# Inner order of the four products per contraction step in a two-feature-tile product (one core)

## The chip, the cores and the metric

The kernel runs on one core of a Trainium2 chip. The metric is the device time in microseconds, the median of the runs.

## The reference, cut to what matters

All arrays are float32. The model has 256 tokens of width 2048. Two layers of attention and MLP come first, then one layer with a recurrent unit (LRU) and a matrix LSTM, then one state-space (SSD) layer. The large products are the input projections and the MLP's first product:

```python
for l in range(DEPTH):                                   # DEPTH = 2
    h = rmsnorm(x, norm_mix[l]);  proj = einsum('bsd,de->bse', h, w_in[l])
    ...                                                  # three attentions
    x = x + einsum('bse,ed->bsd', mix, w_o[l])
    h = rmsnorm(x, norm_mlp[l]);  u = relu(einsum('bsd,df->bsf', h, w_up[l]))
    x = x + einsum('bsf,fd->bsd', u * u, w_down[l])      # u * u: 8192 wide
...
u = x @ w_in                                             # LRU + mLSTM layer
...
u = x @ w_in                                             # SSD layer
```

## The kernel before, in words

**Split operands.** Every float32 factor of a large product is kept as a high part and a low part, both in the engine's float32r form. A product is the sum high x high + high x low + low x high. The weights come from memory as units of 1 MB (`raw`, 128 x 2048), issued by the SyncE queue. ScalarE writes their high part (`whi`), VectorE the low part (`wlo`, line 1590 or 1597). Each of these tiles has four slots. TensorE then multiplies.

**The products of this change** (lines 2639 and 2641 in `products`, lines 2699 and 2701 in `feature_part`) have the weights as the stationary operand and the activations as the moving one. Call them H and L. One pass makes 256 output features, as two feature tiles f = 0, 1 of 128 each. Tile f has its own PSUM bank b + f. The contraction over 2048 has 16 steps kt of 128. In each step and for each f there are two products:

- H: the weights' high part, 128 x 128, against 512 columns: the 256 tokens of the activations' high part, and beside them the 256 of the low part. It fills the whole bank.
- L: the weights' low part, 128 x 128, against the 256 columns of the activations' high part. It is added to the second half of the same bank.

So a step has four products, each with a stationary operand of its own: H0, L0, H1, L1. The next step begins with H0 again. One unit of weights holds eight steps, so a pass uses two units and two slots. Ahead of each unit TensorE waits for `lo_ready` once. After its last L it raises `multiplied`. After the second unit VectorE empties both banks (from line 2180), while TensorE goes on in the other pair of banks. In the first pass of some stages there are also waits ahead of a step (`act_ready`, `x_low`) and small transposes behind it (`turn`, `turn_raw`). In `feature_part` a call of `side` stands behind every second step. It does small pieces of attention. TensorE works strictly in the order in which the lines stand, and the loops over passes are loops on the chip.

`products` does w_up of both layers, the input projections of the last two layers and the products of the SSD groups. `feature_part` does a part of w_in of the two attention layers.

**Other products** have the activations as the stationary operand and 512 columns of weights as the moving one. They come as three products per step and token half, into one bank (lines 2597 to 2599, and the same pattern at 2675, 2738, 3094, 3187 and 3224). One more group of products stands at lines 3019 to 3021 in the mLSTM part: three products of 256 columns each, all into one half of one bank.

Of the kernel before, what the change touches and what calls it, by code (L numbers as in the profile page):

```python
# [21 lines left out]
P = 128  # L22
S = 256
# [9 lines left out]
GC = 256  # L33
# [27 lines left out]
class Own:  # L61
# [9 lines left out]
    def wait(self):  # L71
        self.eng.wait_ge(self.sem, self.n + self.ahead)
# [220 lines left out]
def build(nc, A, out, pick=None):  # L293
# [3 lines left out]
    with ExitStack() as ctx:  # L297
        sems = {}

        def sem(name):  # L300
            if name not in sems:
                sems[name] = ctx.enter_context(nc.semaphore(name))
            return sems[name]

        def sb(name, shape, dt=F32, c=None):
            return (c or ctx).enter_context(nc.sbuf_tensor(name, shape, dt))
# [10 lines left out]
        wlo = sb("wlo", [P, SLOTS, TK * GC], F32R)  # L317
        whi = sb("whi", [P, SLOTS, TK * GC], F32R)
# [32 lines left out]
        act0 = sb("act0", [P, KT, 2, S], F32R)  # L351
# [24 lines left out]
        ps = ctx.enter_context(nc.psum_tensor("ps", [P, 8, 512], F32))  # L376
# [2140 lines left out]
        def _(pe):  # L2517
            T = Tally()

            def turn(i):  # L2520

                wait(pe, sem("act_ready"), T["act_ready"] - 8 + i - 3)
                for kt in range(2):
                    for th in range(2):
                        at = P * (2 * i + kt)
                        ins = pe.matmul(ps[:, 4 + i % 4, kt * S + th * P:kt * S + th * P + P], x[:, th, at:at + P],
                                        xdiag[:, th, :], start=True, stop=True)
                ins.then_inc(sem("x_turned"), 1)

            def turn_raw(i, base):  # L2530

                wait(pe, sem("x_low"), base + i - 3)
                for kt in range(2):
                    for th in range(2):
                        at = P * (2 * i + kt)
                        ins = pe.transpose(ps[:, 4 + i % 4, kt * S + th * P:kt * S + th * P + P], x[:, th, at:at + P],
                                           ident[:, :])
                ins.then_inc(sem("raw_turned"), 1)
# [80 lines left out]
            def products(s, p, c, a, fresh=None):  # L2619

                G = s["G0"] + c
                b = 2 * (G % 2)

                early = s.get("after_resid") and isinstance(p, int) and p == 0 and c == 0
                wait(pe, sem("evacuated"), G - 2 if early else G + 2 * p - 1)
                for j in range(2):
                    slot = 2 * (G % 2) + j
                    pe.wait_ge(sem("lo_ready"), 2 * (G + 2 * p) + j + 1)
                    for i in range(TK):
                        kt = TK * j + i  # L2630
                        if fresh and isinstance(p, int) and p == 0 and c == 0 and kt % fresh == 0:

                            pe.wait_ge(sem("act_ready"), T["act_ready"] - (KT - kt) // fresh + 1)
                        late = s.get("turned") and isinstance(p, int) and p == 0 and c == 0
                        if late and kt % 2 == 0:
                            pe.wait_ge(sem("x_low"), T["x_low"] - 6 + kt // 2 + 1)
                        for f in range(2):
                            w = slice(i * GC + f * P, i * GC + f * P + P)
                            pe.matmul(ps[:, b + f, :], whi[:, slot, w], a[:, kt, :, :].rearrange("p a t -> p (a t)"),  # L2639
                                      start=(kt == 0), stop=False)  # L2640
                            ins = pe.matmul(ps[:, b + f, S:2 * S], wlo[:, slot, w], a[:, kt, 0, :],  # L2641
                                            start=False, stop=(kt == KT - 1))
                        if s.get("turns") and isinstance(p, int) and p == 0 and c == 0 and kt < 8 and kt % 2:
                            turn(4 + kt // 2)
                        if late and kt in (3, 5):
                            pe.wait_ge(sem("evacuated"), G)
                            turn_raw(6 + kt // 5, T["x_low"] - 6)
                    ins.then_inc(sem("multiplied"), 1)

            for s in plan:  # L2650
                k = s["kind"]
                if k == "attn":
                    l, H, Q, U = s["l"], 32 * s["l"], 16 * s["l"], 2 * s["G0"]

                    def bank(k):

                        return 2 * ((s["G0"] + k) % 2)
# [32 lines left out]
                    def feature_part(i, k, n, side):  # L2690

                        u = U + i
                        slot, b = u % SLOTS, bank(k)
                        pe.wait_ge(sem("lo_ready"), u + 1)
                        for a in range(TK):
                            kt = TK * n + a
                            for f in range(2):
                                w = slice(a * GC + f * P, a * GC + f * P + P)
                                pe.matmul(ps[:, b + f, :], whi[:, slot, w], act0[:, kt, :, :].rearrange("p a t -> p (a t)"),  # L2699
                                          start=(kt == 0), stop=False)  # L2700
                                ins = pe.matmul(ps[:, b + f, S:2 * S], wlo[:, slot, w], act0[:, kt, 0, :],  # L2701
                                                start=False, stop=(kt == KT - 1))
                            if a == TK - 1:
                                ins.then_inc(sem("multiplied"), 1)
                            if a % 2:
                                side(4 * i + a // 2)
# [177 lines left out]
                    def side(t):  # L2884

                        if t == 28:
                            make_row()
                        if t in (175, 179, 183):
                            p = (t - 175) // 4
                            pe.wait_ge(sem("evacuated"), s["G0"] + 19 + p + 1)  # L2890
                            if p == 0:
                                pe.wait_ge(sem("g_std"), 3 * l + 3)
                                pe.wait_ge(sem("mixed"), Q + 16)
                            turn_raw(2 * p, X1)
                            turn_raw(2 * p + 1, X1)
                        if t in ROPE_TURN:
                            rope_turn(ROPE_TURN.index(t))
                        if t == KA_TURN:
                            keys_turn()
                        if t in SUMS_AT:  # L2900
                            group_sums(SUMS_AT.index(t))
                        if t in S_AT:
                            scores(S_AT.index(t))
                        if t in T_AT:
                            turn_probs(T_AT.index(t))
                        if t in V_AT:
                            head_values(V_AT.index(t))
# [40 lines left out]
                if k == "norm":  # L2948
                    d = T["diag"]
                    T.done(**counts(s))  # L2950
                    for th in range(2):
                        pe.wait_ge(sem("diag"), d + th + 1)
                        for i in range(4):
                            wait(pe, sem("act_ready"), T["act_ready"] - 8 + i - 3)
                            for kt in range(2):
                                at = P * (2 * i + kt)
                                ins = pe.matmul(ps[:, 4 + i, kt * S + th * P:kt * S + th * P + P], x[:, th, at:at + P],
                                                xdiag[:, th, :], start=True, stop=True)
# [32 lines left out]
                if k == "e_mix":  # L2991
# [117 lines left out]
                    for k in range(32):  # L3109
                        low = k < 16  # L3110
                        p, n = (k // 4, k % 4) if low else m_passes(k - 16)
                        b = 2 * ((e_G0 + p) % 2)
# [9 lines left out]
                        if k == 31:  # L3122
                            for th in range(2):
                                for u, m in ((U + 42, 2), (U + 43, 3)):
                                    slot = u % SLOTS
                                    pe.wait_ge(sem("lo_ready"), u + 1)
                                    pe.wait_ge(sem("ym_low"), m + 1)
                                    for a in range(4):
                                        kt = 4 * m + a
# [4 lines left out]
                                        ins = pe.matmul(to, ym_lo[:, kt, rows], hi, start=False, stop=(kt == KT - 1))  # L3134
# [10 lines left out]
                        if k == 1:  # L3145
                            pe.wait_ge(sem("m_rows"), 1)
                            pe.wait_ge(sem("vtok_in"), 4)
                            for st in range(2):
                                ins = pe.transpose(ps[:, 6, 4 * st:4 * st + 4], rstd[0:4, 1, st * P:st * P + P],
                                                   ident[0:4, 0:4])  # L3150
# [18 lines left out]
                if k == "ssd_out":  # L3169
                    g = s["g"]  # L3170
                    done = {}
                    for i, (p, n) in enumerate(passes(s)[0:12]):
                        u, b = 2 * s["G0"] + i, 2 * ((s["G0"] + p) % 2)
# [7 lines left out]
                        slot = u % SLOTS  # L3181
                        for a in range(4):
                            kt = 4 * n + a
                            hi, lo = whi[:, slot, 512 * a:512 * a + 512], wlo[:, slot, 512 * a:512 * a + 512]
                            for th in range(2):
# [3 lines left out]
                                ins = pe.matmul(ps[:, b + th, :], a_lo, hi, start=False, stop=(last and a == 3))  # L3189
# [12 lines left out]
                    for i, (th, p) in enumerate(OUT_ORDER):  # L3202
                        b, slot = 2 * ((s["G0"] + p) % 2), (2 * s["G0"] + 12 + p) % SLOTS
# [4 lines left out]
                        if i == 7:  # L3208
                            for c in range(2):
                                to = ps[:, b + 1 - c, 0:256]  # L3210
                                for a in range(4):
# [5 lines left out]
                                    ins = pe.matmul(to, a_lo, hi, start=False, stop=(a == 3))  # L3217
                                ins.then_inc(sem("rows_done"), 1)
                            break
                        for a in range(4):  # L3220
                            kt = 12 + a
# [4 lines left out]
                            ins = pe.matmul(ps[:, b + th, :], a_lo, hi, start=False, stop=(a == 3))  # L3226
# [34 lines left out]
```

## Time and profile before

| | |
|---|---|
| median of 3 runs | 3438.71 us (3438.64 to 3439.45) |
| span of the profiled execution | 3437.4 us |
| TensorE products, busy | 3424.9 us, 18380 instructions |
| TensorE weight loads, busy | 2871.9 us, 18380 instructions |
| VectorE | 2236.8 us, 65% |
| ScalarE | 1600.3 us, 47% |
| GpSimd | 688.6 us, 20% |
| DMA | about half of the 16 engines' time, 183 GB/s |

Matmuls are pipelined, so their records overlap: a product's duration in the profile is longer than the distance from its start to the start of the next. What a product costs is that distance. It is read here as (start of the last - start of the first) / (count - 1) over a long stretch. The weight load of a product is a record of its own (PEld) and lies beside the product ahead of it.

### The profile page before, as it was taken

Reading aid. Unit: us, or ns where it says so; the run is one execution under the profiler, and the core shown is the slowest. Engines: PE = TensorE matmul, PEld = TensorE weight load, DVE = VectorE, ACT = ScalarE, POOL = GpSimd, SP = SyncE. Lnnn points to the kernel's source line nnn. Section 1 sums busy time; section 2 is a strip of 40 time slices with the busy share of each in tenths; the row PEclk is TensorE's granted clock in tenths of the full one; section 3 lists DMA queues with packets and bytes.
Section 4 is the critical chain, followed back from the end, with each engine's and each line's share of the span. In section 5 each row is a group of like instructions: output and inputs, shape, how many; then the busy total and the mean of one; then the engine's idle time right before and its main releaser. Section 6 shows DMA issues by size and latency. Waiting matters only on the chain.

```text
span 3437.4 us, 45081 instructions
## 1 busy us (share of the span) xinstructions
PE 3424.9 (100%) x18380; PEld 2871.9 (84%) x18380; DVE 2236.8 (65%) x2182; ACT 1600.3 (47%) x1787; POOL 688.6 (20%) x595
## 2 busy tenths in 40 slices
PE   9999999999999999999999999999999999999999
PEld 7888888888888888888888888888888888888887
DVE  6667646464655667646464657876767575885786
ACT  5555334333344555334333345744454444664564
POOL 1231000000000231000000000391000059773660
PEclk9999999999999999999999999999999999999999
DMA  6354555555555454555555555555444455554554
GB/s 234 139 190 164 194 184 189 191 183 187 189 184 183 146 190 160 187 193 183 190 188 184 184 197 185 182 184 185 183 166 163 169 180 190 194 195 176 186 203 153
DMA packets 95935, 627.90 MB, mean 183 GB/s; under 512 B 11564, under 2 KB 13868, under 8 KB 22672
## 3 DMA queue, kind: packets, MB, share of 16 engines
q1 hardware_dynamic: 84176, 601.92, 48.7%
q0 software_dynamic: 4096, 12.47, 1.4%
q10 hardware_dynamic: 7488, 11.01, 1.0%
q8 instruction: 129, 2.11, 0.2%
q14 instruction: 46, 0.38, 0.0%
HBM read 621.09 MB, written 2.17 MB: 181 GB/s over the span
## 4 chain that ended last, share of the span: by engine, by line
PE 99%; DMA 0%; ACT 0%; SPq 0%; DVE 0%; issue 0%; ACTq 0%; DVEq 0%
PE ps L2639 30%; PE ps L2641 15%; PE ps L2597 8%; PE ps L2599 8%; PE ps L2598 8%; PE ps L2699 3%; PE ps L2738 2%; PE ps L2739 2%; PE ps L2740 2%; PE ps L2675 2%; PE ps L3095 2%; PE ps L2676 2%; PE ps L3096 2%; PE ps L3094 2%; PE ps L2677 2%; PE ps L2701 1%
## 5 line engine op out<-in xcount | busy, mean ns | idle before, releaser
L2639 PE MATMUL ps<-act,whi 128*128 128x512 f32 x4384 | 1550.9, 396 | 0.7 <-DVE act L1829 0.7
L2641 PE MATMUL ps<-act,wlo 128*128 128x256 f32 x4384 | 1234.0, 281 | 0.0
L1590 DVE TENSOR_TENSOR wlo<-raw,whi 128x2048 fp32r<-128x2048 f32 x400 | 931.1, 2350 | 455.0 <-ACT whi L1072 410.8
L2639 PEld LDWEIGHTS ps<-act,whi 128*128 128x128 f32 x4384 | 824.1, 188 | 198.5 <-issue 2.9
L1072 ACT ACTIVATE whi<-raw 128x2048 fp32r<-128x2048 f32 x342 | 652.8, 1913 | 522.7 <-DMA raw<-in_w_down 305.0
L2641 PEld LDWEIGHTS ps<-act,wlo 128*128 128x128 f32 x4384 | 822.8, 188 | 0.7
L953 ACT ACTIVATE whi<-raw 128x2048 fp32r<-128x2048 f32 x226 | 430.9, 1913 | 273.2 <-DMA raw<-in_o_w_in 97.1
L1597 DVE TENSOR_TENSOR wlo<-raw,whi 128x2048 fp32r<-128x2048 f32 x168 | 394.8, 2354 | 126.1 <-ACT whi L953 126.1
L2597 PE MATMUL ps<-whi,act 128*128 128x512 f32 x1152 | 455.9, 396 | 0.0
L2599 PE MATMUL ps<-whi,act 128*128 128x512 f32 x1152 | 455.0, 395 | 0.0
L2598 PE MATMUL ps<-wlo,act 128*128 128x512 f32 x1152 | 455.0, 395 | 0.0
L2597 PEld LDWEIGHTS ps<-whi,act 128*128 128x128 f32 x1152 | 216.2, 188 | 53.0 <-DVE wlo L1590 0.4
L2599 PEld LDWEIGHTS ps<-whi,act 128*128 128x128 f32 x1152 | 216.2, 188 | 52.6
L2598 PEld LDWEIGHTS ps<-wlo,act 128*128 128x128 f32 x1152 | 216.2, 188 | 51.8
L1377 ACT ACTIVATE act<-big 128x512 f32 (+1 forms) x64 | 40.4, 632 | 425.6 <-DVE big L2194 425.6
L2180 DVE COPY big<-ps 128x512 f32<-128x512 f32 x93 | 64.3, 692 | 167.5 <-PE ps L2641 167.4
L785 POOL DMA_DIRECT2D wide_b<-in_bias_b x4 | 2.3, 570 | 794.2 <-DVE wide L1869 794.2
L2699 PE MATMUL ps<-act,whi 128*128 128x512 f32 x384 | 138.7, 401 | 0.0
L864 POOL DMA_DIRECT2D wide_b<-in_norm_final x1 | 0.6, 593 | 663.2 <-PE ps L2641 663.2
L752 POOL TENSOR_SCALAR wide<-wide_b,head 128x256 f32<-128x256 f32 x96 | 111.5, 1172 | 3.1
L747 POOL TENSOR_SCALAR wide<-wide_b,head 128x256 f32<-128x256 f32 x48 | 45.9, 962 | 313.8 <-DVE wide_b L2189 119.3
L2701 PE MATMUL ps<-act,wlo 128*128 128x256 f32 x384 | 107.9, 281 | 0.0
(477 smaller groups left out, 4510.0 us busy)
## 6 DMA issues: line engine op xcount, KB each, us to landing
raw<-in_w_up SPq DMA_DIRECT2D x128, 1024.0 KB, 4.8
raw<-in_w_down SPq DMA_DIRECT2D x128, 1024.0 KB, 4.8
raw<-in_o_w_in SPq DMA_DIRECT2D x80, 1024.0 KB, 4.8
raw<-in_e_w_in SPq DMA_DIRECT2D x64, 1024.0 KB, 4.8
raw<-in_w_in SPq DMA_DIRECT2D x59, 1024.0 KB, 4.8
raw<-in_w_o SPq DMA_DIRECT2D x32, 1024.0 KB, 4.8
raw<-in_e_w_out SPq DMA_DIRECT2D x32, 1024.0 KB, 4.8
raw<-in_o_w_out SPq DMA_DIRECT2D x32, 1024.0 KB, 4.8
```

The source lines that it names most:

```text
L752: own.sign(pool.tensor_scalar(tap[:, a, :], src[:, a, :], columns[:, at:at + 1], 0.0, ALU.mult, ALU.add))
L953: act.activation(whi[:, slot, :], raw[:, slot, :], ACT.Copy).then_inc(sem("hi_ready"), 1)
L1072: act.activation(whi[:, slot, :], raw[:, slot, :], ACT.Copy).then_inc(sem("hi_ready"), 1)
L1590: dve.tensor_tensor(wlo[:, slot, :], raw[:, slot, :], whi[:, slot, :].bitcast(F32), ALU.subtract).then_inc(sem("lo_ready"), 1)
L1597: dve.tensor_tensor(wlo[:, slot, :], raw[:, slot, :], whi[:, slot, :].bitcast(F32), ALU.subtract).then_inc(sem("lo_ready"), 1)
L2597: pe.matmul(ps[:, b + th, :], a_hi, hi, start=(kt == 0), stop=False)
L2598: pe.matmul(ps[:, b + th, :], a_hi, lo, start=False, stop=False)
L2599: ins = pe.matmul(ps[:, b + th, :], a_lo, hi, start=False, stop=(kt == KT - 1))
L2639: pe.matmul(ps[:, b + f, :], whi[:, slot, w], a[:, kt, :, :].rearrange("p a t -> p (a t)"), start=(kt == 0), stop=False)
L2641: ins = pe.matmul(ps[:, b + f, S:2 * S], wlo[:, slot, w], a[:, kt, 0, :], start=False, stop=(kt == KT - 1))
L2699: pe.matmul(ps[:, b + f, :], whi[:, slot, w], act0[:, kt, :, :].rearrange("p a t -> p (a t)"), start=(kt == 0), stop=False)
L2701: ins = pe.matmul(ps[:, b + f, S:2 * S], wlo[:, slot, w], act0[:, kt, 0, :], start=False, stop=(kt == KT - 1))
```

## The change

In each contraction step both products of 512 columns come first and then both of 256: H0, H1, L0, L1 in the place of H0, L0, H1, L1. The same edit is made in `products` and in `feature_part`. Each product keeps its operands, its PSUM columns and its start and stop flags. The semaphore increment stays on the last product of the unit, which is L1 in both orders.

```diff
+                        cols = [slice(i * GC + f * P, i * GC + f * P + P) for f in range(2)]
                         for f in range(2):
-                            w = slice(i * GC + f * P, i * GC + f * P + P)
-                            pe.matmul(ps[:, b + f, :], whi[:, slot, w], a[:, kt, :, :].rearrange("p a t -> p (a t)"),
-                                      start=(kt == 0), stop=False)
-                            ins = pe.matmul(ps[:, b + f, S:2 * S], wlo[:, slot, w], a[:, kt, 0, :],
+                            pe.matmul(ps[:, b + f, :], whi[:, slot, cols[f]],
+                                      a[:, kt, :, :].rearrange("p a t -> p (a t)"), start=(kt == 0), stop=False)
+                        for f in range(2):
+                            ins = pe.matmul(ps[:, b + f, S:2 * S], wlo[:, slot, cols[f]], a[:, kt, 0, :],
                                             start=False, stop=(kt == KT - 1))
```

## Rows read from the trace of the kernel before

**Rows 1.** The page: parts 1 and 4, engines' busy time, and the chain that ended last.
```profile
PE 3424.9 (100%) x18380; PEld 2871.9 (84%) x18380; DVE 2236.8 (65%) x2182; ACT 1600.3 (47%) x1787; POOL 688.6 (20%) x595
PE 99%; DMA 0%; ACT 0%; SPq 0%; DVE 0%; issue 0%; ACTq 0%; DVEq 0%
PE ps L2639 30%; PE ps L2641 15%; PE ps L2597 8%; PE ps L2599 8%; PE ps L2598 8%; PE ps L2699 3%; PE ps L2738 2%; PE ps L2739 2%; PE ps L2740 2%; PE ps L2675 2%; PE ps L3095 2%; PE ps L2676 2%; PE ps L3096 2%; PE ps L3094 2%; PE ps L2677 2%; PE ps L2701 1%
```

**Rows 2.** Groups of instructions by line: count, busy us, mean ns, idle before.
```profile
L2639 PE MATMUL ps<-act,whi 128*128 128x512 f32 x4384 | 1550.9, 396 | 0.7 <-DVE act L1829 0.7
L2699 PE MATMUL ps<-act,whi 128*128 128x512 f32 x384 | 138.7, 401 | 0.0
L2641 PEld LDWEIGHTS ps<-act,wlo 128*128 128x128 f32 x4384 | 822.8, 188 | 0.7
```

**Rows 3.** H in six stretches: us, PE busy (count), PEld busy (count), clock, DMA.
```profile
330.00:414.00 84.00, 84.00 (x241) 45.15 (x241) 1.00 0.52 188
504.00:593.00 89.00, 88.98 (x256) 47.82 (x255) 1.00 0.53 189
690.00:770.00 80.00, 80.00 (x227) 42.48 (x227) 1.00 0.53 188
505.00:585.00 80.00, 80.00 (x231) 43.16 (x230) 1.00 0.53 191
1363.00:1447.00 84.00, 84.00 (x241) 45.17 (x241) 1.00 0.52 188
1537.00:1626.00 89.00, 89.00 (x256) 47.84 (x255) 1.00 0.53 189
```

**Rows 4.** Timeline of PE: first and last H of 690 to 770, then of 505 to 585.
```profile
689.95 0.39 PE L2639 MATMUL ps<-act,whi 128*128 128x512 f32 x1
...
769.79 0.40 PE L2639 MATMUL ps<-act,whi 128*128 128x512 f32 x1
...
504.67 0.40 PE L2639 MATMUL ps<-act,whi 128*128 128x512 f32 x1
...
584.91 0.39 PE L2639 MATMUL ps<-act,whi 128*128 128x512 f32 x1
```

**Rows 5.** Only long products: count of L2597 from 420 to 500, its first and last.
```profile
420.00:500.00 80.00, 44.93 (x115) 21.43 (x115) 1.00 0.52 186
419.62 0.39 PE L2597 MATMUL ps<-whi,act 128*128 128x512 f32 x1
...
499.42 0.39 PE L2597 MATMUL ps<-whi,act 128*128 128x512 f32 x1
```

**Rows 6.** Only short products, L3019: two stretches with counts, then first and last of each.
```profile
2456.00:2466.00 10.00, 7.84 (x30) 5.37 (x29) 1.00 0.58 210
2467.50:2472.40 4.90, 4.00 (x15) 2.66 (x15) 1.00 0.60 216
2455.74 0.28 PE L3019 MATMUL ps<-act,whi 128*128 128x256 f32 x1
...
2465.99 0.28 PE L3019 MATMUL ps<-act,whi 128*128 128x256 f32 x1
...
2467.45 0.28 PE L3019 MATMUL ps<-act,whi 128*128 128x256 f32 x1
...
2472.21 0.28 PE L3019 MATMUL ps<-act,whi 128*128 128x256 f32 x1
```

**Rows 7.** Timeline: a short product behind another kind of work, and the next one.
```profile
2467.01 0.39 PE L3019 MATMUL ps<-act,whi 128*128 128x256 f32 x1
2467.23 0.28 PE L3020 MATMUL ps<-act,whi 128*128 128x256 f32 x1
```

**Rows 8.** Timeline of products and loads around one L: who lies beside whom.
```profile
760.85 0.28 PE L2641 MATMUL ps<-act,wlo 128*128 128x256 f32 x1
760.85 0.19 PEld L2639 LDWEIGHTS ps<-act,whi 128*128 128x128 f32 x1
760.97 0.39 PE L2639 MATMUL ps<-act,whi 128*128 128x512 f32 x1
760.97 0.19 PEld L2641 LDWEIGHTS ps<-act,wlo 128*128 128x128 f32 x1
```

**Rows 9.** Who waited for whom: VectorE, then the SyncE queue, from 690 to 770.
```profile
DVE big L2180 <- PE ps L2641: 14.6, 7, 2.2
SPq L678 <- PE ps L2641: 70.8, 14, 5.3
```

More of the change, by code:

```diff
@@ L2696, in feature_part @@
                             kt = TK * n + a
+                            cols = [slice(a * GC + f * P, a * GC + f * P + P) for f in range(2)]
                             for f in range(2):
[L2698 to L2701, printed above, removed]
+                                pe.matmul(ps[:, b + f, :], whi[:, slot, cols[f]],
+                                          act0[:, kt, :, :].rearrange("p a t -> p (a t)"), start=(kt == 0), stop=False)
+                            for f in range(2):
+                                ins = pe.matmul(ps[:, b + f, S:2 * S], wlo[:, slot, cols[f]], act0[:, kt, 0, :],
                                                 start=False, stop=(kt == KT - 1))
```

## Prediction

> **What bounds the kernel now.** First the page's chain of work and its busy times: the chain is 99% TensorE, whose products fill the span, while VectorE has 65% and ScalarE 47% [rows 1]. Next the groups by line: the 4384 H of line 2639 were preceded by 0.7 us of idle time in all [rows 2], so no engine and no transfer holds TensorE up in this part. Last the waits of the others: in one stretch VectorE's copy and the DMA queue both wait for L of line 2641 [rows 9]. They run behind TensorE. So only one thing counts, the distance from the start of a product to the start of the next. The four lines of the change hold 30 + 15 + 3 + 1 = 49% of the chain [rows 1], some 1680 us. There are (4384 + 384) / 2 = 2384 steps of four products [rows 2]. A step costs about 704 ns. An effect of 0.2%, about what a measurement of this kernel can tell from no change, is 6.9 us, or 2.9 ns per step. That is less than one part in 200 of a step, so the distances must be read to a nanosecond. I do this by dividing long stretches by their counts.
>
> **Two cadences.** From 690 to 770 us 227 H started within 769.79 - 689.95 = 79.84 us, or 353.3 ns for each pair H, L. From 505 to 585 us it was 231 H in 80.24 us, or 348.9 ns [rows 3, 4]. Granted clock (1.00, the 2.4 GHz level), DMA share (0.53) and instructions are the same in both. A step thus costs 706.6 or 697.8 ns. I call these the slow and the fast cadence. Once started, either one lasts over a whole stage. Four long stretches are fast, 241 + 256 + 241 + 256 = 994 of 4768 pairs [rows 3]. With the shorter fast pieces in the same view I count 28%. The mean is 0.28 x 697.8 + 0.72 x 706.6 = 704.1 ns.
>
> Products of 512 columns alone come at (499.42 - 419.62) / 114 / 3 = 233.3 ns [rows 5]. Products of 256 columns alone come at 10.25 / 29 / 3 = 117.8 ns in one stretch and at 4.76 / 14 / 3 = 113.3 ns in another [rows 6]. So the short products have a slow and a fast cadence too, and 4.5 ns lie between them, about as in the pairs (4.4). I match slow with slow and fast with fast.
>
> **The change, part by part.**
>
> *Order of the lengths.* Before, the length changes four times per step (H L H L), after it twice (H H L L). What does such a change cost? Slow: a pair takes 353.3, its two members alone take 233.3 + 117.8 = 351.1. Fast: 348.9 against 233.3 + 113.3 = 346.6. Both leave 2.2 to 2.3 ns per pair, so about 1.1 ns per change of length. In the new step two changes remain: slow 353.3 + 233.3 + 117.8 = 704.4, fast 348.9 + 233.3 + 113.3 = 695.5. Either way the step saves 2.2 ns. 2384 x 2.2 = 5.2 us. No row shows H H L L, so this is bounded from both sides. At best nothing is lost at the changes and the cadence is always fast: 466.6 + 226.6 = 693.2, which is 10.9 ns less than 704.1, or 26 us. At worst see the slower rival. I take 2.2 because both cadences give it.
>
> *Weight loads.* Every product needs its own stationary operand in either order (high f = 0, high f = 1, low f = 0, low f = 1). Nothing is kept across two products, and the count of loads stays at 18380 [rows 1]. The load of a product starts with the product ahead of it: at 760.85 both L and the load for the next H, which starts at 760.97 [rows 8]. So before, the four covers are H, L, H, L. After, they are again two long and two short ones: H0 covers the load of H1, H1 that of L0, L0 that of L1, and L1 that of the next H0. A short cover of 113.3 ns is enough for three short products in a row [rows 6], although the load's record is 188 ns long [rows 2]. I cost this at zero. If the cover were gone, a load would cost about 2467.23 - 2467.01 - 0.113 = 0.11 us, as behind the other kind of work [rows 7].
>
> *PSUM.* Before, L is added to the bank that H wrote just ahead of it. After, another bank lies between. Lines 2597 to 2599 write one bank three times running and then change it, at the same 233.3 ns on average [rows 5]. Within a bank the order stays H, then L. Cost zero, and nothing to gain either.
>
> *Waits and queues.* `lo_ready`, `act_ready` and `x_low` stand ahead of the step, and `turn` and `side` behind it, as before. No instruction passes them. `multiplied` is still on L1, so VectorE's copy, ScalarE's next high part and the DMA queue are released at the same place in the stream [rows 9]. If TensorE became faster by 0.3%, they would have to follow. VectorE at 65% can [rows 1].
>
> **Sum.** In the profiled execution: span 3437.4 - 5.2 = 3432.2 us. The median of the runs is 1.3 us above that span, so 3438.7 - 5.2 = 3433.5 us.
>
> **The rivals.**
>
> *More of the fast cadence.* Which cadence a stage gets changes at stalls and at changes of the pattern, without any difference in work that I can see. A new pattern may fall into another. If all steps were fast: 704.1 - 695.5 = 8.6 ns, times 2384 = 20.5 us, so 3418 us. If all were slow: 704.4, so +0.7 us, 3439.4 us. For it: a slow share of 72% leaves far more room below than above. Against: nothing in the rows says why a stage is fast.
>
> *The order does not count.* Each product costs by its length alone, and the 2.2 ns per pair are the lengths' own. Then the time stays at 3438.7 us. Against it: both cadences show an excess of the mixed pair over its members.
>
> The Trainium skill, "TensorE: Matmul & The Clock Gate", section "Back-to-back issue gap", gives such a rule: columns / 2.4 + 2.5 ns when warm, that is 216 ns for 512 columns and 109 for 256. By it the step is the same in both orders and the sum is zero. The rows disagree with its sizes (233.3, and 113.3 to 117.8), so I give this less weight than the forecast.
>
> *Slower: two short products in a row cost at both ends.* The mechanism: what is lost at a change of length grows with the short run, because the second short product and the H0 behind it get their loads under short covers, one after the other. The place is the start of L1 and of the next H0. The price: suppose all steps keep the slow cadence and each change costs 4.4 ns in place of 1.1. Then the step is 466.6 + 235.6 + 8.8 = 711.0 ns, 6.9 more than 704.1, so +16.4 us, 3455 us. It decides from 707.1 ns per step on, or 2.4 ns per change of length. For it: no row has a run of exactly two short products ahead of a long one. Against: runs of three and more are at 117.8 or less [rows 6], and the pair of before has a short cover ahead of each H.
>
> The same page, section "LDWEIGHTS (loading the stationary operand)", puts a load at columns / 1.2, that is 107 ns for 128 columns. The fast short cadence of 113.3 [rows 6] leaves 6 ns over it. By that page a run of short products just covers its loads, and the sum would not change.
>
> **How the numbers follow.** Forecast, 2.2 ns per step with the cadences mixed roughly as now: 0.42. Its own range is 3429 to 3438 us, a quarter of it beyond 0.2%. More of the fast cadence, 3418: 0.30. Order does not count, 3438.7: 0.15. Slower, 3455: 0.13. So faster by over 0.2% (under 3431.8): 0.30 + 0.42 / 4 = 0.40. Within 0.2%: 0.32 + 0.15 = 0.47. Slower (over 3445.6): 0.13. The range runs from 3414, near the best bound (3412.5), up into the slower case, 3447 us. Some 0.06 is left out below and 0.1 above.
>
> **What would show it right or wrong.** In the changed kernel H0 to H0 of the next step should be 704 or 696 ns, read as above over a w_up stage. TensorE must still have no idle time at these lines, and 18380 loads. A step of 693 to 696 throughout is the fast rival. Over 707 throughout is the slower one, and then the distance behind the second L should stand out against that behind the first. If H0 to H0 is as forecast and the total is not, other lines moved, and those at 2597 to 2599 are the first to look at. The prediction is wrong most easily in the shares of the two cadences, which I carry over and do not explain.

## The result, and the profile after

The changed kernel takes 3412.57 us (median of 5, 3411.59 to 3416.99) against 3439.15 us before. The ratio is 0.9924, with a 95% interval of 0.9913 to 0.9935. That is 26.6 us less, where 5.2 us were forecast. The time lies just under the lower end of the range, 3414.

The page of the changed kernel, parts 1 and 5. It answers to [rows 1, 2]. Columns of the groups: line, engine, operation, count, then busy us, mean ns, idle time before.

```profile
span 3415.2 us, 45081 instructions
PE 3395.1 (99%) x18380; PEld 2859.8 (84%) x18380; DVE 2239.2 (66%) x2182; ACT 1600.0 (47%) x1787; POOL 693.2 (20%) x595
...
L2639 PE MATMUL ps<-act,whi 128*128 128x512 f32 x4384 | 1365.9, 393 | 6.8 <-DVE wlo L1590 6.0
...
L2642 PE MATMUL ps<-act,wlo 128*128 128x256 f32 x4384 | 865.7, 279 | 0.0
```

The counts are those of before, the 18380 weight loads too. The records of these two lines are nearly as long as before (393 and 279 ns against 396 and 281), so little is seen by looking at one record. What changed is the distance between starts. The fall of "busy" (L from 1234.0 to 865.7) is no gain of that size either. Records overlap, and two short ones that overlap each other cover less time.

The distance, over the two w_up stages that had the fast and the slow cadence before. First the windows for line 2639 (us, PE busy and count), then the timeline of TensorE at both ends. "x2" is a pair H0, H1.

```profile
515.17:584.86 69.69, 62.71 (x202) 30.59 (x203) 1.00 0.53 192
700.00:764.86 64.86, 58.35 (x188) 28.47 (x189) 1.00 0.52 186
```

```profile
515.20 0.62 PE L2639 MATMUL ps<-act,whi 128*128 128x512 f32 x2
515.66 0.40 PE L2642 MATMUL ps<-act,wlo 128*128 128x256 f32 x2
...
584.90 0.62 PE L2639 MATMUL ps<-act,whi 128*128 128x512 f32 x2
...
700.04 0.62 PE L2639 MATMUL ps<-act,whi 128*128 128x512 f32 x2
...
764.90 0.62 PE L2639 MATMUL ps<-act,whi 128*128 128x512 f32 x2
```

In the first stretch 202 H are 101 steps in 584.90 - 515.20 = 69.70 us, 690 ns each. In the second it is 94 steps in 64.86 us, 690.0 ns. Before, the same stages took 697.8 and 706.6 ns [rows 3, 4]. The slow cadence has gone, and the step is shorter than the fast one too. In the whole trace, unbroken groups of twelve steps have a median of 690.0 ns. Granted clock (1.00) and DMA share are unchanged. From a mean of 704.1 that is 14.1 ns per step. If all 2384 steps gained it, that would be 33.6 us.

I also added up, over the whole trace, the distances from each start at the four lines to the next product's start: 1689.6 us before, 1658.6 after, 31.0 less. So the steps that other work interrupts gained a little less than 14.1 ns. Everything else grew by 8.7 us. What is left is the 22.2 us between the two spans. The profiled execution was the longest of the five (3416.99 us), so the medians lie 26.6 us apart and not 22.2. The 31.0 us come back in every trace with the changed order: the four lines add up to 1658.5 to 1658.8 us in the kernel above, its repeat, e2, e3, e4, e8, e10 and e15. What varies is the rest.

Part of that rest is waiting. TensorE now waits where it did not. Who waited for whom, TensorE, the changed kernel:

```profile
PE ps L2639 <- DVE wlo L1590: 6.0, 10, 1.4
PE ps L2579 <- POOL osum L766: 1.8, 3, 0.6
PE ps L2536 <- DMA x<-in_x: 1.7, 1, 1.7
```

The first two lines are new, 7.8 us together. One of the waits in the timeline (start, us, engine, line; idle time before in brackets):

```profile
2913.74 5.59 DVE L1590 TENSOR_TENSOR wlo<-raw,whi 128x2048 fp32r<-128x2048 f32 x2
...
2916.17 0.47 PE L2639 MATMUL ps<-act,whi 128*128 128x512 f32 x1 [1.42 <-DVE wlo L1590]
```

This is an SSD group. VectorE writes the low parts of the weights only behind two instructions of the group's own work (line 1650), and each of these waits for ScalarE. VectorE, the changed kernel, ahead of the same wait:

```profile
2904.03 0.69 DVE L1609 TENSOR_TENSOR wide_b<-ps,wide_b 128x512 f32<-128x512 f32 x1
2911.10 0.96 DVE L1650 TENSOR_TENSOR big<-big,rstd 128x768 f32<-128x768 f32 x1 [6.38 <-ACT big L988]
2912.86 0.96 DVE L1650 TENSOR_TENSOR sq<-sq,rstd 128x768 f32<-128x768 f32 x1 [0.80 <-ACT sq L988]
```

So VectorE had not run out of time: it stood idle for 6.38 us just before. The same sequence, with an idle time of 1.3 us or more at its head, stands ahead of all eight waits for line 1590 in these groups. It was there before the change too, with hardly any time to spare (the kernel before, VectorE and then TensorE at the same place of another group):

```profile
2970.88 1.12 DVE L1650 TENSOR_TENSOR big<-big,rstd 128x768 f32<-128x768 f32 x1 [1.34 <-ACT big L988]
2972.64 1.91 DVE L1650 TENSOR_TENSOR sq<-sq,rstd 128x768 f32<-128x768 f32 x1 [0.64 <-ACT sq L988]
2974.47 4.68 DVE L1590 TENSOR_TENSOR wlo<-raw,whi 128x2048 fp32r<-128x2048 f32 x2
...
2977.00 0.50 PE L2639 MATMUL ps<-act,whi 128*128 128x512 f32 x1
```

The first of the two low parts ended at 2976.75, and H started 0.25 us later. At this place in five of the groups the distance was 0.18 to 0.42 us before. In the changed kernel H starts 0.15 us behind the end of the low part in the same five, after a wait of 0.36 to 0.41 us.

### The profile page after: what moved, and what is told of

Same layout as the page of the kernel before. It is cut to its first block and busy times, and to the rows that moved or that the text cites. A ratio compares the mean times of both kernels' runs of the same rounds, so it can differ in the third digit from the quotient of the medians.

```text
span 3415.2 us, 45081 instructions
## 1 busy us (share of the span) xinstructions
PE 3395.1 (99%) x18380; PEld 2859.8 (84%) x18380; DVE 2239.2 (66%) x2182; ACT 1600.0 (47%) x1787; POOL 693.2 (20%) x595
## 5 line engine op out<-in xcount | busy, mean ns | idle before, releaser
L2639 PE MATMUL ps<-act,whi 128*128 128x512 f32 x4384 | 1365.9, 393 | 6.8 <-DVE wlo L1590 6.0
L2642 PE MATMUL ps<-act,wlo 128*128 128x256 f32 x4384 | 865.7, 279 | 0.0
L2639 PEld LDWEIGHTS ps<-act,whi 128*128 128x128 f32 x4384 | 665.5, 188 | 11.2 <-issue 9.8
L2597 PE MATMUL ps<-whi,act 128*128 128x512 f32 x1152 | 456.3, 396 | 0.1
L2599 PE MATMUL ps<-whi,act 128*128 128x512 f32 x1152 | 455.4, 395 | 0.0
L2597 PEld LDWEIGHTS ps<-whi,act 128*128 128x128 f32 x1152 | 216.5, 188 | 52.1 <-DVE wlo L1590 0.5
L2700 PE MATMUL ps<-act,whi 128*128 128x512 f32 x384 | 122.1, 399 | 0.0
L747 POOL TENSOR_SCALAR wide<-wide_b,head 128x256 f32<-128x256 f32 x48 | 50.9, 1066 | 312.0 <-DVE wide_b L2189 118.9
L2676 PE MATMUL ps<-whi,act 128*128 128x512 f32 x256 | 103.6, 405 | 0.5 <-DVE act L1763 0.4
```

The lines of the kernel that those rows point to most:

```text
L2597: pe.matmul(ps[:, b + th, :], a_hi, hi, start=(kt == 0), stop=False)
L2639: pe.matmul(ps[:, b + f, :], whi[:, slot, cols[f]], a[:, kt, :, :].rearrange("p a t -> p (a t)"), start=(kt == 0), stop=False)
L2642: ins = pe.matmul(ps[:, b + f, S:2 * S], wlo[:, slot, cols[f]], a[:, kt, 0, :], start=False, stop=(kt == KT - 1))
L2676: pe.matmul(ps[:, b + th, :], a_hi, hi, start=(kt == 0), stop=False)
L2700: pe.matmul(ps[:, b + f, :], whi[:, slot, cols[f]], act0[:, kt, :, :].rearrange("p a t -> p (a t)"), start=(kt == 0), stop=False)
```

## The experiments

Of e1 to e9, and of e13 and e14, there is one execution each, and it is the traced one. What counts in them is the step, read as above over a long stretch. The two cadences of before come out alike, to 0.1 ns, in the same long stages of three traces (before, e1 and e7). Three theories stood against each other at first. Bank theory: a product costs less when it lands in another PSUM bank than the product ahead of it. Shared theory: two neighbours that read the same moving operand cost less. Run theory: what counts is how often the length changes. A fourth, tile theory, came with e7: a product costs more when its stationary operand is in another tile than its neighbour's.

**e1: order of before, every product in another bank.**

```diff
-                        for f in range(2):   # H0 H1, then L0 L1
+                        for f in range(2):
+                            to_h, to_l = (b, b + 1) if 0 < kt < KT - 1 else (b + f, b + f)
+                            pe.matmul(ps[:, to_h, :], whi[...], ...)
+                            ins = pe.matmul(ps[:, to_l, S:2 * S], wlo[...], ...)
```

> The order of before, H0 L0 H1 L1, but for steps 1 to 14 of the 16 both H go to the first bank and both L to the second, so that every product lands in another bank than the one ahead of it. This mixes the two feature tiles, so the sums differ from the reference's. Bank theory (a product costs less when it lands in another bank than the product ahead of it): H0 to the next H0 about 690 ns as in the changed kernel, about 3415 us. Run theory (fewer changes of length) and shared theory (the moving operand of two neighbours is the same): the length still changes four times and no two neighbours read the same columns, so 698 or 707 ns as before, about 3438 us.

Measured: 3438.7 us beside 3438.3 for the kernel before. Windows and timeline, e1, slow stage:

```profile
700.00:764.66 64.66, 64.66 (x184) 34.40 (x184) 1.00 0.52 188
699.67 0.40 PE L2640 MATMUL ps<-act,whi 128*128 128x512 f32 x1
...
764.34 0.40 PE L2640 MATMUL ps<-act,whi 128*128 128x512 f32 x1
```

184 H, from the first start to the last 64.67 us, are 353.4 ns per pair, 706.7 per step, and in the fast stage it is 697.8. Both cadences of before are there again. A change of bank at every product buys nothing.

**e2: changed order, all in one bank.**

```diff
+                        to = [b, b if 0 < kt < KT - 1 else b + 1]
-                            pe.matmul(ps[:, b + f, :], ...)
+                            pe.matmul(ps[:, to[f], :], ...)
```

> The changed order, H0 H1 L0 L1, but for steps 1 to 14 all four products go to one bank, which mixes the two feature tiles. Bank theory: 700 ns or more per step, about 3438 us or above. Run theory and shared theory: 690 ns, about 3415 us.

Measured: 3415.0 us.

```profile
700.26:764.43 64.17, 57.67 (x188) 28.17 (x186) 1.00 0.51 185
699.97 0.62 PE L2640 MATMUL ps<-act,whi 128*128 128x512 f32 x2
...
764.14 0.62 PE L2640 MATMUL ps<-act,whi 128*128 128x512 f32 x2
```

94 pairs, 93 steps in 64.17 us: 690.0 ns, all in one bank. With e1, the bank theory has fallen from both sides.

**e3: changed order, neighbours read different moving operands.**

```diff
+                        skew = (0, 1 - 2 * (kt % 2))     # f = 1 takes the steps of each two in the other order
-                                      a[:, kt, :, :]...
+                                      a[:, kt + skew[f], :, :]...
```

> The changed order and its banks, but the second feature tile works through each two neighbouring contraction steps in the other order, so that H0 and H1, and L0 and L1, never read the same moving operand. Bank theory and run theory: 690 ns, about 3415 us. Shared theory: back to 698 to 707 ns, about 3438 us.

Measured: 3412.8 us, 690.0 ns per step. The shared theory has fallen.

**e4: block products, bank changes at every product.**

```diff
-                        for th in range(2):
-                            ... a_hi * hi; a_hi * lo; a_lo * hi
+                        for m, (e, w) in enumerate(((0, hi), (0, lo), (1, hi))):
+                            for th in range(2):
+                                ins = pe.matmul(ps[:, b + th, :], parts[th][e], w, ...)
```

> The changed kernel, and in its other kind of product (block_products, six products of 512 columns per step) the two token halves alternate, so that the bank changes at every product instead of every third one and the pairs share their moving operand. Bank theory: six of these products fall from 1400 ns to about 6 x 228 = 1368, 1152 of 32 ns, 37 us in all, less what TensorE then waits for. Shared theory: a gain too, half of it or all. Run theory: no change of length here before or after, 1400 ns, 0 us.

Measured: 3412.4 us. Six of these products still take 1400 ns. No gain from banks or from a shared moving operand here either. Only the run theory had said so.

**e6: runs of four.** The orders, not the code:

```diff
-   H0 H1 L0 L1 | H0' H1' L0' L1'
+   H0 H1 H0' H1' L0 L1 L0' L1'
```

> The changed kernel carried on: two contraction steps together, four long products and then four short ones (H0 H1 H0' H1' L0 L1 L0' L1'), so the length changes once per step in place of twice. Run theory, with each change of length costing the same: from two changes per step to one saves as much again as from four to two (14 ns), so about 676 ns per step, about 3380 us before new waits. Rival (the run of two is a favourable pattern, longer runs go back to what products of one length cost, 466.6 + 226.6 to 235.6): 693 to 702 ns, 3420 to 3440 us. Tile theory (below): stationary operands alternate even less, 690 ns or under.

Measured: 3420.0 us beside 3440.0 before.

```profile
700.98:764.61 63.63, 49.84 (x185) 31.23 (x185) 1.00 0.51 185
700.89 1.07 PE L2641 MATMUL ps<-act,whi 128*128 128x512 f32 x4
...
764.52 1.07 PE L2641 MATMUL ps<-act,whi 128*128 128x512 f32 x4
```

46 x 4 + 1 H, so 46 double steps in 63.63 us: 1383.3 ns, 691.7 per step. That is more than with runs of two, not 14 ns less. The run theory in its simple form, one price for each change of length, is wrong as well. My rival said 693 to 702 and missed too, though by little.

**e7 and e8: the tile of the stationary operand.** In e7 the order is that of before with one tile, in e8 the changed order with the tiles in turn.

```diff
 e7                         pe.matmul(ps[:, b + f, :], whi[...], ...)
-                           ins = pe.matmul(ps[:, b + f, S:2 * S], wlo[...], ...)
+                           ins = pe.matmul(ps[:, b + f, S:2 * S], whi[...], ...)
 e8                         weights = (whi, wlo)       # by feature tile f
-                           whi[:, slot, cols[f]]  and  wlo[:, slot, cols[f]]
+                           weights[f][:, slot, cols[f]]  in both
```

> The order of before, H0 L0 H1 L1, but L takes its stationary operand from the tile of the high parts too, so all four products read one tile. That leaves the low parts of the weights out of these products. Tile theory (a product costs more when its stationary operand comes from another tile than that of the product ahead): 690 ns or less per step, about 3412 us. Run theory: 698 or 707 ns as before, about 3438 us.

> The changed order of lengths, H0 H1 L0 L1, but the stationary operands come from the tiles high, low, high, low in turn (the second feature tile uses the low parts throughout, the first the high parts, so the sums are not the reference's). Tile theory: 698 to 707 ns, about 3438 us. Run theory: 690 ns, about 3413 us.

Measured: e7 3441.5 us beside 3440.0 before, with both cadences of before, 697.8 and 706.7. e8 3412.1 us, 690.0. The tile theory has fallen. What is left of the seven runs is the order of the lengths.

**e9: four equal lengths.**

```diff
+                        h, l = (384, 384) if kt else (512, 256)
-   512 512 256 256 columns
+   384 384 384 384 columns
```

> From the second contraction step on, all four products have 384 columns in place of 512, 512, 256, 256: the same 1536 columns per step, no change of length at all. The low part of the activations counts for half of the tokens only and part of the high part is used otherwise, so the sums are not the reference's. Run theory: at most 690 ns, less if each change costs 7 ns (676). Rival (a stream of one length has a cadence of its own, as 512 columns at 233.3 ns and 256 at 113.3 to 117.8): in between, 4 x 173.3 to 175.5 = 693 to 702 ns.

Measured: 3418.8 us.

```profile
700.09:764.53 64.44, 48.04 (x187) 33.24 (x188) 1.00 0.52 190
700.08 0.51 PE L2640 MATMUL ps<-act,whi 128*128 128x384 f32 x2
...
764.51 0.51 PE L2640 MATMUL ps<-act,whi 128*128 128x384 f32 x2
```

93 steps in 64.43 us: 692.8 ns. One step in sixteen, the first of each pass, still has the old lengths. Where all steps are equal the trace has 693.3 ns. No change of length at all, and still 3.3 ns more than the changed order. This is the rival's side, at its lower edge. Three uniform streams now stand on a line: 256 columns at 113.3 (the fast ones of [rows 6]), 384 at 173.3, 512 at 233.3 [rows 5]. Each 128 columns more cost 60 ns, and a product costs 6.7 ns less than 60 ns for each 128 of its columns. So four products with 1536 columns together make 693.3 ns by this line, whatever their lengths.

**e13 and e14: one product alone.** Again the orders, not the code:

```diff
-   H H L L H H L L
+   H H L H H L L L          (e13: one short product alone)
+   H L L H H H L L          (e14: one long product alone)
```

> Two contraction steps together in the order H H L H H L L L: one short product stands alone between long ones, no long one stands alone. Members alone give 1386 ns in the fast cadence. From the runs so far I take -3.3 ns for each short run of two or more, and +2.3 (fast) to +6.8 ns (slow) for a short one alone in H L H L. Short-alone theory (the lone short product costs): 1386.5 - 3.3 + 2.3 to 6.8 = 1385 to 1390 ns per two steps. Long-alone theory (the lone long product costs, the lone short one does not): 1386.5 - 6.7 = 1380 ns. Total about 3418 us by the first, 3413 by the second.

> The mirror of it: H L L H H H L L, one long product alone between short ones, no short one alone. Short-alone theory: 1380 ns per two steps. Long-alone theory: 1385 to 1390 ns.

Measured: e13 3427.2 us, e14 3418.3 us beside 3439.4 before. Windows and timeline, first e13, then e14:

```profile
700.26:764.51 64.25, 55.41 (x185) 28.00 (x185) 1.00 0.54 195
700.14 0.62 PE L2644 MATMUL ps<-act,whi 128*128 128x512 f32 x2
...
764.38 0.62 PE L2644 MATMUL ps<-act,whi 128*128 128x512 f32 x2
```

```profile
700.09:763.87 63.78, 57.43 (x185) 31.30 (x184) 1.00 0.54 192
699.94 0.39 PE L2644 MATMUL ps<-act,whi 128*128 128x512 f32 x1
...
763.73 0.39 PE L2644 MATMUL ps<-act,whi 128*128 128x512 f32 x1
```

Both have 46 double steps: 64.24 us or 1396.5 ns in e13 (1396.7 over the whole trace), 63.79 us or 1386.7 ns in e14. The lone short product is the worse one, by 10 ns, so the direction of the short-alone theory holds. Its numbers do not: it said 1385 to 1390 and 1380, and both came out 7 ns higher or more. A lone long product costs something as well, or a run of three does: e13 has three short ones in a row and e14 three long ones, and no run separates the two readings.

**e10, e12 and e15: the pattern carried to the block products**, with four executions each. e10 splits the third of each three products into halves, e12 does it at seven places, e15 changes the neighbours.

```diff
-                            ins = pe.matmul(ps[:, b + th, :], a_lo, hi, ...)
+                            for c in (slice(0, 256), slice(256, 512)):
+                                ins = pe.matmul(ps[:, b + th, c], a_lo, hi[:, c], ...)
 e15: both hi*hi | both lo*hi, first half | both hi*lo | both lo*hi, second half
```

> The changed kernel, and in block_products the third product of each three is split into two halves of 256 columns, each with its own load of the same stationary operand. The lengths are then 512 512 256 256 over and over, the pattern of the changed step, at 8 products in place of 6 and the same 3072 columns. Pattern theory (the distance is set by the sequence of lengths alone, whatever bank, tile or operand): 2 x 690 = 1380 ns per contraction step in place of 1400, 576 steps, 11.5 us less: about 3401 us, less what TensorE then waits for. Rival (each product and each load has a price of its own, so two more of them per step cost more): 1400 ns plus two times 3 ns or more, 3416 us or above.

> The same split at all seven places that have three products of 512 columns in a row (lines 2599, 2678, 2742, 3098, 3136, 3191 and 3228 of the changed kernel), some 1020 steps of six. Pattern theory: 1020 x 20 ns = 20 us less than the changed kernel, about 3393 us, less new waits in the attention and mixing stages, where small work stands between. Rival of prices per product: slower than the changed kernel by 6 us or more.

> Block products split as before into 512 512 256 256, but the two token halves alternate: both high x high, then the first halves of both low x high, then both high x low, then the second halves. So no two neighbours have the same stationary operand, and neighbours go to different banks. If two neighbours with one stationary operand were the reason for 1387 ns: 1380 ns per contraction step, 3.8 us less than with the plain split, about 3405 us. If not: 1387 ns, about 3409 us.

Measured: e10 3408.9 us (3406.3 to 3410.4), e12 3407.6 (3405.7 to 3410.7), e15 3407.3 (3406.3 to 3408.1). Ratios to before are 0.9909 (0.9893 to 0.9926), 0.9908 (0.9892 to 0.9925) and 0.9905 (0.9889 to 0.9922). The changed kernel, measured beside e10 and e12, took 3416.3. Windows and timeline, e10, line 2597 (the first of each three):

```profile
430.57:488.81 58.24, 32.59 (x85) 15.77 (x84) 1.00 0.57 197
430.34 0.39 PE L2597 MATMUL ps<-whi,act 128*128 128x512 f32 x1
...
488.58 0.39 PE L2597 MATMUL ps<-whi,act 128*128 128x512 f32 x1
```

84 threes in 58.24 us: 693.3 ns each, so 1386.7 per contraction step, against 1400 [rows 5]. More products and more loads in less time: they have no positive price each, and that rival has fallen. But it is not 1380 either. And 693.3 is just what the prices of the uniform streams give: 2 x 233.3 + 2 x 113.3, where three of 512 columns are 700.0. So the gain of e10 needs no effect of the order at all, and it is no support for the pattern theory. The same sequence of lengths takes 690.0 in one place and 693.3 in the other, so the lengths are not the whole of it. e15 gave 1386.7 again, so two neighbours with one stationary operand are not the reason. e12 was to gain 20 us and got about 9. In its extra places the pattern runs at 1387 as well, with small work between, and the time cannot be told from that of e10.

**e11: the order of before in the SSD groups only**, and the changed kernel again beside it.

```diff
+                        for f, low in (((0, 0), (0, 1), (1, 0), (1, 1)) if s["kind"] == "ssd" else
+                                       ((0, 0), (1, 0), (0, 1), (1, 1))):
```

> The changed kernel itself, beside the ones of this call on the same chip: 690.0 ns per step, 3412 to 3417 us.

> The changed kernel, but in the SSD groups (7 x 4 passes x 16 = 448 of the 2384 steps) the order of before, H0 L0 H1 L1. If what TensorE gained there (448 x 14 ns = 6.3 us) was given back as waits for the weights' low parts (6.0 us in the profile of the changed kernel, most of it in these groups), the time stays within 2 us of the changed kernel and the waits of line 2639 for line 1590 fall under 1 us. If the waits have another cause, they stay and the time rises by about 6 us.

Measured: changed again 3416.3 us (3415.0 to 3418.5), e11 3417.4 (3415.2 to 3418.9), with overlapping ranges. TensorE's waits from 2870 to 3330 us, first changed again, then e11:

```profile
PE ps L2639 <- DVE wlo L1590: 3.3, 6, 1.4
PE ps L2579 <- POOL osum L766: 2.4, 5, 0.7
```

```profile
PE ps L2644 <- DVE wlo L1590: 1.4, 1, 1.4
PE ps L2579 <- POOL osum L766: 0.4, 1, 0.4
```

By the distances added up over the trace, the products of the four lines take 6.8 us longer in e11 and all the rest 5.3 us less. The traces alone would not settle it, since the rest varies from 1743.0 to 1748.4 us among five traces that have the changed order and the other products as they were. The medians do: e11 is 1.0 us over the changed kernel, where 6.8 would be expected if nothing were given back. So in the SSD groups most of the gain is spent. The detail missed: I expected the waits for line 1590 under 1 us, and over the whole of e11 2.7 us remained, of which 1.4 us here.

## Why the prediction was wrong, point by point

**What bounds the kernel: right.** The gain came from the distance between starts at the four lines, 31.0 us, and reading it by stretches and counts was fine enough. But TensorE did not stay free of waits, and all else grew by 8.7 us in the profiled execution.

**Order of the lengths: the sign was right, the size was not.** This is the step that failed. It took the distance as a sum: a price for each member, from stretches of one length, slow matched with slow, and a price for each change of length, from the pairs. The sum gave 2.2 ns, the measurement 14.1. In the changed order the step is below its members even in their fast cadence (690.0 against 693.3).

The trace of before already spoke against such prices. Its fast cadence, three H of it:

```profile
509.90 0.40 PE L2639 MATMUL ps<-act,whi 128*128 128x512 f32 x1
510.13 0.28 PE L2641 MATMUL ps<-act,wlo 128*128 128x256 f32 x1
510.25 0.39 PE L2639 MATMUL ps<-act,whi 128*128 128x512 f32 x1
510.48 0.28 PE L2641 MATMUL ps<-act,wlo 128*128 128x256 f32 x1
510.60 0.39 PE L2639 MATMUL ps<-act,whi 128*128 128x512 f32 x1
```

From 515 to 580 us the distance behind an H is 230.0 ns on average and behind an L 118.9. The long product is 3.3 ns under its price alone (233.3), and the short one 5.6 over (113.3). The 2.3 ns per pair were the difference of the two, not a cost of two changes. In the slow cadence the two distances are 233.3 and 120.1, in the changed order 228.8 and 116.2 (both from 700 to 764 us). So both kinds of product gained.

Nor does a price per change of length fit. In e6 the step is 691.7, with half as many changes. In e13 and e14, with as many changes as the changed order, it is 698.3 and 693.3. Per 1536 columns, with four products (the last two lines three and six, from [rows 5, 6]):

| lengths in turn | ns |
|---|---|
| H L H L (before, e1, e7) | 697.8 or 706.7 |
| H H L H H L L L (e13) | 698.3 |
| H L L H H H L L (e14) | 693.3 |
| four of 384 (e9) | 693.3 |
| H H L L in the block products (e10, e12, e15) | 693.3 |
| H H H H L L L L (e6) | 691.7 |
| H H L L (changed, e2, e3, e8) | 690.0 |
| 512 columns alone, three products | 700.0 |
| 256 columns alone, six products | 680 or 707 |

The Trainium skill, "TensorE: Matmul & The Clock Gate", section "Back-to-back issue gap", gives columns / 2.4 + 2.5 ns as the gap of an isolated product at the 2.4 GHz clock. Carried over to this stream, as the prediction's rival did, its form would make the first seven lines equal. The measurements differ by up to 17 ns, so here they decide against it.

**The lower bound was no bound.** The "best" case of 693.2 ns was built from streams of one length. Nothing said that a mixed stream can't run better, and it does. Of the 14.1 ns, 10.9 lie within that case (the slow cadence gone, nothing lost at the changes) and 3.2 beyond it. The range was also cut off above its own bound: 704.1 - 693.2 = 10.9 ns are 26.0 us, so 3412.7 us (the text has 3412.5), and the range began at 3414. The result, 3412.6, lies next to that bound only by luck: the step gained more than the bound allows, and what grew elsewhere took the excess back.

**The rival "more of the fast cadence".** I gave it 0.30 and 3418 us. Its direction was right: the slow cadence is gone in every stage. But the changed order does not fall into one of the two old cadences. It has one of its own, at the same 690.0 ns in every long stage. The forecast's own range (3429 to 3438) rested on carrying the old shares over. That was the assumption named as the weakest, and it failed. The rival's ground was also not chance: in before, e1 and e7 the same long stages are fast (those from 328 and 504 us) and the same are slow (from 682 and 862), and in the second layer it is so again.

**Weight loads and PSUM: cost zero, right.** 18380 loads as before. e1 and e2 show no effect of the banks here, in either order. The slower rival, loads under two short covers, did not appear: the step became shorter, not longer.

**Waits and queues: wrong in the SSD groups.** I judged VectorE by its mean of 65% over the span ("VectorE at 65% can"). Its share in the stretch of these groups would not have told more: it is three quarters in both kernels. All engines from 2870 to 3330 us, before and then changed:

```profile
2870.00:3330.00 460.00, 459.99 (x2591) 389.80 (x2590) 341.87 (x290) 249.62 (x311) 294.75 (x238) 1.00 0.53 189
```

```profile
2870.00:3330.00 460.00, 453.15 (x2565) 384.72 (x2564) 346.22 (x299) 253.26 (x317) 281.18 (x225) 1.00 0.53 188
```

What decided was the order of work on VectorE, behind ScalarE, and that only 0.18 to 0.42 us were between the low part and its H at five places. 7.8 us of new waits stand in the profile of the changed kernel, 6.7 of them in these groups. e11 shows that most of the gain of these groups is spent.

**What stays open.** Why the sequence of lengths sets the distance. The runs exclude the PSUM bank, the shared moving operand, the tile of the stationary operand, the number of loads and the number of changes. The orders with a short product alone between long ones have the longest steps (697.8 to 706.7 and 698.3), though e13 leaves the run of three short ones as another reading. The runs do not show the mechanism. Nor do they show why before had two cadences, or why 512 512 256 256 takes 690.0 in one kind of product and 693.3, the sum of the uniform prices, in the other.

## What to carry to other kernels

Where TensorE is the bound and products of different lengths alternate, try grouping them in pairs of equal length. It changes no operand and no count. Here it gave 2% of the step (704.1 to 690.0). Prices from streams of one length missed the new step by 5.5 to 14.4 ns (695.5 and 704.4 against 690.0), more than the 2.2 ns that were forecast from them. Measure the distance between starts over a hundred products or more, not the length of a record. And before counting on a gain in TensorE, measure at each hand-over how long ahead of its product the operand is finished. A busy share, of the span or of the stage, does not show it: VectorE stood idle for 6.4 us and TensorE still had to wait for it.

## What the runs showed of the hardware that I had not expected

A stream of products can have two cadences with the same instructions, clock and DMA share (348.9 or 353.3 ns per pair), each lasting over a whole stage, while another order of the same products has one. Which stage gets which is the same in three traces. The periods come out very exact: 1380.0, 1383.3 and 1386.7 ns per eight products in e2, e6 and e14. In e13 they alternate between about 1392.7 and 1400.7, with 1396.7 as the mean. The first three differ by multiples of 3.33 ns, but the fast cadence of before, 1395.6, does not fit such a grid. And of three products of 512 columns, one split into two of 256, with one load more, makes the stream faster (693.3 against 700.0 ns per 1536 columns), although it adds an instruction pair. Streams of 256, 384 and 512 columns alone cost 113.3, 173.3 and 233.3 ns per product: 6.7 ns less per product than 60 ns for each 128 columns.
